# Two PEER layers on one core: routing weights through a DRAM table instead of one-hot products

## The chip, the cores and the metric

One core of one Trainium2 chip runs the whole network as a single program. The metric is the device time of that program in microseconds (us). The engines are TensorE (PE, matrix products into PSUM), VectorE (DVE), ScalarE (ACT), GpSimd (POOL) and SyncE (SP, which only issues transfers); sixteen DMA engines move data between DRAM and the on-chip memory. Each engine runs its own instructions in order and waits on semaphores that others raise.

## The reference, cut to what matters

The network has six large blocks. The change touches the two PEER blocks (`l` = 0 and 1), each a layer of 16384 one-neuron experts of which every token uses 8 x 16:

```python
# 256 tokens, d = 1024, 8 heads, 128 x 128 = 16384 experts, top 16
s1 = einsum('phd,nd->phn', q[..., :half], subkeys[0])
s2 = einsum('phd,nd->phn', q[..., half:], subkeys[1])
v1, i1 = top_k(s1, 16);  v2, i2 = top_k(s2, 16)
cs, ci = top_k((v1[..., :, None] + v2[..., None, :]).reshape(..., 256), 16)
e = take(i1, ci // 16) * 128 + take(i2, ci % 16)        # expert number
g = softmax(cs)                                          # routing weight
a = gelu(einsum('pd,phkd->phk', xb, u_tab[e]))
y = einsum('phk,phkd->pd', g * a, v_tab[e])
```

Neither kernel gathers experts. Both compute the products of every token with all 16384 rows of `u_tab`, apply gelu, multiply by a table of routing weights that is zero for experts not chosen, and multiply the result by all of `v_tab`.

## The kernel before

**The stream.** The tables come from DRAM as slabs of 128 x 2048 floats (1 MB, two halves or tiles of 512 KB), in the order of a fixed plan: among others `gla_v`, `gla_og`, `gla_out` (4 slabs each), `peer_q0` (8), `u0` (64), `v0` (64), and later the same for layer 1. SP loads them into a ring of two slabs; a half is loaded again once its low part has been made (semaphore `lo_made`). One u slab holds 2 x 128 experts, one v slab likewise.

**Products in parts.** Each tile is split into a high and a low part: ACT makes `split_hi` (L1562), DVE or POOL makes `split_lo` = tile - high (L1587 or L1575). PE multiplies high x high, high x low and low x high. There are two buffers of each part, so a maker can be two tiles ahead of PE at most.

**The u stage, 64 slabs.** For slabs 0 to 31 POOL makes the low parts, because DVE is choosing experts at that time (`peer_choose_vector`): the top 16 of each key half, of their sums, the expert numbers, the softmax. PE's lines are L1505 and L1509. For slabs 32 to 63 DVE makes the low parts and PE runs L1529 and L1533; the two halves of each product are copied out by ACT (L1628), added by DVE (L1877, `u_sum_vector`) and put through gelu by ACT. The results fill `gate`, 128 partitions x (128 key rows x 256 tokens).

**The routing weights.** They are built for groups of 8 tokens. DVE compares the chosen key numbers with all key numbers (L1831, L1833: one-hots of rows and columns) and multiplies the row one-hots by the weight in three bf16 parts (L1837, three instructions). PE multiplies column one-hots by weighted row one-hots (`routes_group_tensor`, L1948: 8 tokens x 3 parts = 24 matmuls of 64 columns), into PSUM. DVE multiplies that into `gate` (`routes_merge_vector`, L1848). 32 groups build the first 64 key rows, one group in each of u slabs 32 to 63; 32 more build the other 64 rows, one in each of v slabs 0 to 31.

**The v stage, 64 slabs.** For each tile ACT makes `gate_hi` (L1559) and `split_hi`, DVE makes `gate_lo` (L1585) and `split_lo` (L1587), and PE adds 12 matmuls of 512 columns (L2003). In slabs 32 to 63 DVE also computes four strips of modulation vectors for later blocks from 512 KB loads that POOL issues (`strip_chunk_vector`, L356; loads L395, two buffers `mod_w`), one chunk per slab nearly.

**Who waits for whom.** PE waits on ACT and DVE by counters (`hi_made`, `lo_made`, `gate_lo_made`), they on PE (`hi_free`, `lo_free`).

Of the kernel before, what the change touches and what calls it, by code (L numbers as in the profile page):

```python
# [29 lines left out]
I32 = mybir.dt.int32  # L30
# [11 lines left out]
RING = 2  # L42
BANK = 512
# [79 lines left out]

TWO_PI = 6.283185307179586
# [5 lines left out]
def build(nc, io, marks):  # L130

    new_marks = {}
    with ExitStack() as ctx:
# [40 lines left out]
        iota = sb("iota", [P, P])  # L174

# [70 lines left out]
        banks_free = sem("routes_banks_free")  # L246
# [15 lines left out]
        hot_rows, hot_cols = sem("hot_rows"), sem("hot_cols")  # L262
        hot_equal = sem("hot_equal")
        mlp_drained, mlp_squared, hid_made = sem("mlp_drained"), sem("mlp_squared"), sem("hid_made")
        routes_full = sem("routes_full")
# [773 lines left out]
        def constants_gpsimd(g):  # L1039
            for buf, val in ((ident, 0.0), (ones, 1.0), (zeros, 0.0), (band, 0.0), (after, 0.0),  # L1040
                             (blockm, 0.0), (upper, 1.0), (gmask_f, 1.0)):
                nc.gpsimd.memset(buf[:, :], val).then_inc(gpsimd_steps, g.step())
            nc.gpsimd.iota(iota[:, :], pattern=[[1, P]], base=0, channel_multiplier=0,
# [366 lines left out]
        peer_qT = gate[:, 80 * SEQ:(80 + 2 * PEER_H) * SEQ].rearrange("p (g n) -> p g n", g=2 * PEER_H)  # L1410
        A = Area(small)
        e_sel = A.take(3, NT, HK)
        top_v = A.take(2 * PEER_H, TOPK)
        top_if = A.take(2 * PEER_H, TOPK)
        top_i = A.take(2 * PEER_H * TOPK).bitcast(U32).rearrange("p (a b) -> p a b", b=TOPK)
        cand = A.take(TOPK * TOPK)
        cand2 = A.take(TOPK * TOPK)
        c_i = A.take(HK).bitcast(U32)
        c_part = A.take(HK).bitcast(U32)
        c_pf = A.take(HK)  # L1420
        match = A.take(4, TOPK, TOPK)
# [3 lines left out]
        HALF = KEYS // 2  # L1425
        GROUP = 8
        W_PARTS = 3

        def take_bf16(*shape):
            n = int(np.prod(shape))  # L1430
            ap = B.take(n // 2).bitcast(BF16)
            return ap.rearrange("p (a b) -> p a b", a=shape[0]) if len(shape) == 2 else ap
        PAIR = 2
        selT = take_bf16(2 + W_PARTS, SEQ * PAIR).rearrange("p n (t q) -> p n t q", q=PAIR)
        keys_bf = take_bf16(1, KEYS)[:, 0, :]
        hot_c = [take_bf16(GROUP, KEYS) for _ in range(2)]
        hot_r = [[take_bf16(GROUP, HALF) for _ in range(W_PARTS)] for _ in range(2)]
        w_left = B.take(SEQ)
# [38 lines left out]
        def peer_score_tensor(t, l):  # L1477
# [37 lines left out]
            with t.eng.Fori(0, 3) as i:  # L1515
                for j in range(8):
                    u_slab(i, j)
            for j in range(6):
                u_slab(3, j)
            peer_turn_tensor(t, l)  # L1520
            for j in range(6, 8):
                u_slab(3, j)
# [25 lines left out]
            with t.eng.Fori(4, 8) as i:  # L1548
                routed(i)
# [14 lines left out]
        def split_lo_gpsimd(g, name, i0, i1):  # L1564


            g.eng.wait_ge(lo_made, i0 * 8 + TILE0[name])
            with g.eng.Fori(i0, i1) as i:
                for j in range(4):
                    slot = (START[name] + j) % RING  # L1570
                    for e in range(2):
                        tile = TILE0[name] + 2 * j + e
                        g.eng.wait_ge(hi_made, i * 8 + (tile + 1))
                        g.eng.wait_ge(lo_free, i * 8 + (tile + 1))
                        nc.gpsimd.tensor_tensor(split_lo[:, e, :], ring[:, slot, e * D:(e + 1) * D],  # L1575
                                                split_hi[:, e, :].bitcast(F32), ALU.subtract).then_inc(lo_made, 1)
            g.seen.clear()
# [12 lines left out]
        def peer_score_scalar(a, l):  # L1590
# [44 lines left out]
            def late_step(i, first):  # L1635
                for j in range(8):
                    for e in range(2):
                        split_hi_scalar(a, f"u{l}", i, j, e, 8)
                    if j == 0 and first:
                        drain(i - 1, 7)  # L1640
                        continue
                    if j >= 2 or not first:
                        late_gelu(i if j >= 2 else i - 1, (j - 2) % 8)
                    late_copy(i if j else i - 1, (j - 1) % 8)

            def step(i, first=False):
                for j in range(8):
                    for e in range(2):
                        if j or not first:
                            split_hi_scalar(a, f"u{l}", i, j, e, 8)  # L1650
                    if j:
                        drain(i, j - 1)
                    elif not first:
                        drain(i - 1, 7)
                    if j == 4 and isinstance(i, int) and i == 3:
                        a.wait_ge(*when(f"chosen{l}"))
                        w = e_sel[:, 2, :, :].rearrange("p a b -> p (a b)")
                        nc.scalar.activation(w, w, ACT.Exp).then_inc(scalar_steps, a.step(f"weights{l}.exp"))
# [1664 lines left out]
```

## Time and profile before

| | us |
|---|---|
| median of 3 runs (2586.33 to 2589.01) | 2588.92 |
| span of the profiled execution | 2591.7 |
| PE busy | 2514.7 (97%) |
| DVE busy | 2119.7 (82%) |
| ACT busy | 1220.0 (47%) |
| POOL busy | 468.9 (18%) |

The profiled execution's span is 2.8 us above the median of the runs, 0.1%. A busy PE is not a PE at its peak, since its matmuls overlap in a pipeline; what a stage costs is read from the distance between the starts of its slabs. The granted PE clock is 1.00 in all stages from 60 us on that are shown below.

### The profile page before, as it was taken

Reading aid. Unit: us, or ns where it says so; the run is one execution under the profiler, and the core shown is the slowest. Engines: PE = TensorE matmul, PEld = TensorE weight load, DVE = VectorE, ACT = ScalarE, POOL = GpSimd, SP = SyncE. Lnnn points to the kernel's source line nnn. Section 1 sums busy time; section 2 is a strip of 40 time slices with the busy share of each in tenths; the row PEclk is TensorE's granted clock in tenths of the full one; section 3 lists DMA queues with packets and bytes.
Section 4 is the critical chain, followed back from the end, with each engine's and each line's share of the span. In section 5 each row is a group of like instructions: output and inputs, shape, how many; then the busy total and the mean of one; then the engine's idle time right before and its main releaser. Section 6 shows DMA issues by size and latency. Waiting matters only on the chain.

```text
span 2591.7 us, 48983 instructions
## 1 busy us (share of the span) xinstructions
PE 2514.7 (97%) x17184; PEld 2192.0 (85%) x17184; DVE 2119.7 (82%) x3783; ACT 1220.0 (47%) x1769; POOL 468.9 (18%) x385
## 2 busy tenths in 40 slices
PE   5999999999999999999999999999999999999998
PEld 4789999888888877899998888887878789777987
DVE  7889997888888778869978888887777788777754
ACT  4544444545444545444444554444545554334543
POOL 2115992000000001018980000000101000110000
PEclk8999999999999999999999999999999999999999
DMA  9775555555456887365555445546887567964554
GB/s 345 259 263 168 179 178 172 166 166 185 169 167 211 284 271 272 130 220 171 183 179 166 162 166 185 170 168 231 282 286 256 189 222 262 318 242 163 171 183 149
DMA packets 147831, 538.38 MB, mean 208 GB/s; under 512 B 16609, under 2 KB 16865, under 8 KB 147442
## 3 DMA queue, kind: packets, MB, share of 16 engines
q1 hardware_dynamic: 114226, 414.78, 46.9%
q0 software_dynamic: 32752, 119.24, 13.2%
q10 hardware_dynamic: 720, 2.62, 0.3%
q8 instruction: 79, 1.29, 0.2%
q14 instruction: 54, 0.44, 0.1%
HBM read 533.42 MB, written 3.15 MB: 207 GB/s over the span
## 4 chain that ended last, share of the span: by engine, by line
PE 83%; DVE 7%; POOL 3%; issue 3%; DMA 2%; ACT 2%; SPq 0%; DVEq 0%; POOLq 0%; ACTq 0%
PE ps L2003 26%; PE ps L1529 9%; PE ps L2748 7%; PE ps L748 6%; PE ps L1505 6%; PE ps L1457 5%; PE ps L1533 5%; PE ps L2730 5%; PE ps L1948 3%; PE ps L1509 3%; POOL split_lo L1575 3%; PE ps L2734 2%; DVE gate L928 1%; DMA gate<-in_mod 1%; PE ps L2142 1%
## 5 line engine op out<-in xcount | busy, mean ns | idle before, releaser
L1562 ACT ACTIVATE split_hi<-ring 128x1024 fp32r<-128x1024 f32 x760 | 801.0, 1056 | 757.8 <-PE ps L1509 199.8
L1587 DVE TENSOR_TENSOR split_lo<-ring,split_hi 128x1024 fp32r<-128x1024 f32 x572 | 698.5, 1222 | 177.0 <-ACT split_hi L1562 172.2
L1575 POOL TENSOR_TENSOR split_lo<-ring,split_hi 128x1024 fp32r<-128x1024 f32 x128 | 339.9, 2672 | 91.2 <-ACT split_hi L1562 90.9
L1559 ACT ACTIVATE gate_hi<-gate 128x256 fp32r (+1 forms) x252 | 105.4, 418 | 405.4 <-PE ps L2003 398.9
L2003 PE MATMUL ps<-split_hi,gate_hi 128*128 128x512 f32 x1024 | 285.1, 398 | 1.5 <-DVE gate_lo L1585 1.5
L2003 PE MATMUL ps<-split_hi,gate_lo 128*128 128x512 f32 x1024 | 278.2, 392 | 5.1 <-DVE gate_lo L1585 5.0
L2003 PE MATMUL ps<-split_lo,gate_hi 128*128 128x512 f32 x1024 | 278.0, 391 | 0.0
L1505 PE MATMUL ps<-h_parts,split_hi 128*128 128x256 f32 x2048 | 266.9, 283 | 0.0
L1529 PE MATMUL ps<-h_parts,split_hi 128*128 128x512 f32 x1024 | 261.6, 397 | 0.0
L1505 PEld LDWEIGHTS ps<-h_parts,split_hi 128*128 128x128 f32 x2048 | 254.9, 192 | 0.0
L2003 PEld LDWEIGHTS ps<-split_hi,gate_lo 128*128 128x128 f32 x1024 | 192.6, 189 | 48.4 <-DVE gate_lo L1585 7.5
L2003 PEld LDWEIGHTS ps<-split_lo,gate_hi 128*128 128x128 f32 x1024 | 191.8, 188 | 43.6 <-DVE split_lo L1587 3.3
L2003 PEld LDWEIGHTS ps<-split_hi,gate_hi 128*128 128x128 f32 x1024 | 187.7, 189 | 40.6 <-ACT split_hi L1562 2.8
L1529 PEld LDWEIGHTS ps<-h_parts,split_hi 128*128 128x128 f32 x1024 | 183.5, 189 | 32.7
L1585 DVE TENSOR_TENSOR gate_lo<-gate,gate_hi 128x256 fp32r<-128x256 f32 x252 | 106.8, 424 | 113.7 <-ACT split_hi L1562 112.2
L395 POOL DMA_DIRECT2D mod_w<-in_mod x64 | 33.8, 528 | 694.7 <-DVE strip_part L356 688.8
L1533 PEld LDWEIGHTS ps<-h_parts,split_lo 128*128 128x128 f32 x1024 | 139.7, 190 | 10.2
L1509 PE MATMUL ps<-h_parts,split_lo 128*128 128x256 f32 x1024 | 145.1, 284 | 2.0 <-POOL split_lo L1575 2.0
L436 POOL DMA_DIRECT2D small<-in_mod x104 | 55.1, 530 | 490.5 <-DVE modc L356 459.9
L1533 PE MATMUL ps<-h_parts,split_lo 128*128 128x256 f32 x1024 | 142.5, 282 | 0.0
L1837 DVE TENSOR_TENSOR small<-small 128x512 bf16<-128x512 bf16 x384 | 139.7, 421 | 0.0
L356 DVE CUSTOM_DVE_ANT_0 small<-small,gate,cols 128x1024 f32<-128x1024 f32 x104 | 131.9, 1280 | 6.1 <-DMA small<-in_mod 6.1
(405 smaller groups left out, 3951.0 us busy)
## 6 DMA issues: line engine op xcount, KB each, us to landing
ring<-in_stream SPq DMA_DIRECT2D x776, 512.0 KB, 4.3
small<-in_mod POOLq DMA_DIRECT2D x104, 512.0 KB, 5.6
mod_w<-in_mod POOLq DMA_DIRECT2D x64, 512.0 KB, 5.2
gate<-in_mod POOLq DMA_DIRECT2D x44, 512.0 KB, 6.9
gate<-in_mod SPq DMA_DIRECT2D x8, 512.0 KB, 16.2
gate<-in_mod ACTq DMA_DIRECT2D x4, 512.0 KB, 8.3
x_kept<-x POOLq DMA_DIRECT2D x8, 256.0 KB, 3.9
gate<-x_kept POOLq DMA_DIRECT2D x4, 512.0 KB, 8.5
```

The source lines that it names most:

```text
L356: return nc.vector.tensor_tensor_reduce(out=w, in0=w, in1=c_act, scale=1.0, scalar=start, op0=ALU.mult, op1=ALU.add, accum_out=out)
L748: return nc.tensor.matmul(ps[:, banks[2 * nb + i], :], src[:, b * per + n, i * P:(i + 1) * P], w[:, b % 2, at_:at_ + BANK], start=(b == n ...
L1505: nc.tensor.matmul(out, split_hi[:, e, c * P:(c + 1) * P], part[:, c, :], start=(part is hT_hi and c == 0), stop=False)
L1509: ins = nc.tensor.matmul(out, split_lo[:, e, c * P:(c + 1) * P], hT_hi[:, c, :], start=False, stop=(c == DC - 1))
L1529: nc.tensor.matmul(ps[:, bank, :].rearrange("p (a n) -> p a n", a=2), split_hi[:, e, c * P:(c + 1) * P], h_parts[:, :, c, :], start=(c == ...
L1533: ins = nc.tensor.matmul(ps[:, bank, SEQ:2 * SEQ], split_lo[:, e, c * P:(c + 1) * P], hT_hi[:, c, :], start=False, stop=(c == DC - 1), ski ...
L1562: nc.scalar.activation(split_hi[:, e, :], ring[:, slot, e * D:(e + 1) * D], ACT.Copy).then_inc(hi_made, 1)
L1575: nc.gpsimd.tensor_tensor(split_lo[:, e, :], ring[:, slot, e * D:(e + 1) * D], split_hi[:, e, :].bitcast(F32), ALU.subtract).then_inc(lo_m ...
L1587: nc.vector.tensor_tensor(split_lo[:, e, :], ring[:, (START[name] + j) % RING, e * D:(e + 1) * D], split_hi[:, e, :].bitcast(F32), ALU.sub ...
L1837: ins = nc.vector.tensor_tensor(pairs(hot_r[r][m]), equal, of_token(2 + m, HALF), ALU.mult)
L2003: return nc.tensor.matmul(ps[:, 2 * nb + n, :], g[:, e, n * P:(n + 1) * P], w[:, e, nb * BANK:(nb + 1) * BANK], start=opens, stop=True, sk ...
L2748: return nc.tensor.matmul(ps[:, 4 + 2 * nb + n, :], h[:, c0, n * P:(n + 1) * P], w[:, e, nb * BANK:(nb + 1) * BANK], start=(first and h is ...
```

## The change

The weights no longer come from one-hots. For each layer there is a table in DRAM of 128 x 128 experts x 256 tokens (16.8 MB).

- **Clearing.** SP writes zeros from `u_part` into the tables, 16 transfers of 1 MB for each: table 0 between the loads of `gla_v`, `gla_og`, `gla_out` and `peer_q0`, table 1 between the first 34 slabs of `u0`, one after each pair of slabs.
- **Choosing.** DVE chooses in four batches of two heads (both token tiles), not in two of eight. A class `UTiles` puts DVE's low parts between the pieces of choosing by a count of microseconds: no tile in the first 33, then one for each 1.4 (1.0 from tile 64 on). POOL makes the low parts of slabs 0 to 5 only. ACT does the exponentials at slabs 6, 15, 27 and 41 (`EXP_AT`).
- **Adding.** As soon as a batch has weights and row numbers, POOL issues 64 indirect transfers for it (2 heads x 2 token tiles x 16 ranks), each of 128 single floats, one per token, added to the table at the row that an index column in on-chip memory gives. A head waits until the adds of the head before it on the same token tile have landed. 256 of them in each layer.
- **Reading back.** POOL loads the first four slabs of weights (256 KB each), ACT issues the others in the v stage, four ahead. DVE multiplies one slab of weights into `gate` for each v slab, one slab ahead of its use.
- **Strips.** The modulation chunks are spread over the v stage, one for every other slab from slab 2 on.
- PE's one-hot products, DVE's one-hots, the turning of the chosen numbers on PE and the PSUM merges are gone.

The diff, cut to its core:

```diff
+POOL_SLABS, HEAD_START = 6, 33.0
+EXP_AT = [6, 15, 27, 41]
+CLEARS = 16
+FIRST_CLEARS = [START["gla_v"], START["gla_og"], START["gla_out"]]
...
-            def routed(i):
+            def paired(i):
                 for j in range(8):
-                    routes_group_tensor(t, i * 8 + (2 * l * GROUPS + j - GROUPS), j % 2)
...
+        def routes_gpsimd(g, l):
+
+            g.eng.wait_ge(routes_cleared[l], 16 * CLEARS)
+            routes = io["routes"][l].rearrange("a p t -> (a p t)").unsqueeze(1)
+            for b in range(BATCHES):
+                g.wait_ge(*when(f"weights{l}.{b}"))
+                for hh in range(PER):
+                    for i in range(NT):
+                        head = (l * BATCHES + b) * PER + hh
+                        g.wait_ge(routes_added[i], 16 * TOPK * head)
+                        for k in range(TOPK):
+                            n = (i * PER + hh) * TOPK + k
+                            g.eng.indirect_dma_start(
+                                out=routes,
+                                out_offset=bass.IndirectOffsetOnAxis(ap=r_index[:, b, n:n + 1].bitcast(U32), axis=0),
+                                in_=r_weight[:, b, n:n + 1], in_offset=None, compute_op=ALU.add) \
+                                .then_inc(routes_added[i], 16)
+            for i in range(NT):
+                g.wait_ge(routes_added[i], 16 * HK * (l + 1))
+            for slab in range(ROUTE_RING):
+                g.eng.dma_start(route_in[slab], routes_of(l, slab)).then_inc(first_routes_landed, 16)
...
+        class UTiles:
...
+            def after(self, us):
+
+                self.spent += us
+                while self.spent > 0:
+                    share = HEAD_START if self.tile == 2 * POOL_SLABS else 1.4 if self.tile < 64 else 1.0
+                    if self.tile == 2 * POOL_SLABS and self.spent < share:
+                        return
+                    self.one()
+                    self.spent -= share
...
+        def routes_merge_vector(v, l, slab):
+
+            if slab < ROUTE_RING:
+                v.wait_ge(first_routes_landed, 16 * ROUTE_RING * (l + 1))
             else:
...
+                v.wait_ge(route_landed[slab % ROUTE_RING], 16 * (15 * l + slab // ROUTE_RING))
+            v.wait_ge(u_drained, 68 * l + 4 + slab + 1)
+            dst = gate[:, 2 * slab * SEQ:(2 * slab + 2) * SEQ]
+            nc.vector.tensor_tensor(dst, dst, route_in[slab % ROUTE_RING].rearrange("p a t -> p (a t)"), ALU.mult) \
+                .then_inc(routes_merged, 1)
...
+            for slab in range(1, 64):
+                a.wait_ge(routes_merged, 64 * l + slab + 1)
+                if slab + ROUTE_RING < 64:
+                    route_load_scalar(a, l, slab + ROUTE_RING)
                 for e in range(2):
...
+                    if a == START["u0"]:
+                        with sp.Fori(1, 1 + CLEARS) as i:
+                            pair(i)
+                            clear_routes(1, i - 1)
```

How the instructions stand. First PE, in the second half of the u stage, one slab with what stands around it, before (`ps` is PSUM, `h_parts` the tokens' activations, `small` the one-hots):

```order
L1948 MATMUL ps<-small 128x64 x24
L1527 ISA
L1529 MATMUL ps<-h_parts,split_hi 128x512 x8
L1533 MATMUL ps<-h_parts,split_lo 128x256 x8
L1527 REGISTER_ALU
L1529 MATMUL ps<-h_parts,split_hi 128x512 x8
L1533 MATMUL ps<-h_parts,split_lo 128x256 x8
L1943 REGISTER_ALU
```

and now:

```order
L1526 MATMUL ps<-h_parts,split_hi 128x512 x8
L1530 MATMUL ps<-h_parts,split_lo 128x256 x8
L1524 REGISTER_ALU
L1526 MATMUL ps<-h_parts,split_hi 128x512 x8
L1530 MATMUL ps<-h_parts,split_lo 128x256 x8
L1538 REGISTER_ALU
```

The 24 small matmuls are gone from the slab; the 32 large ones stay as they were. The same 24 are gone from v slabs 0 to 31.

Second, POOL in the u stage of layer 0, from its last low part on. Before (the end of the loop that makes 64 tiles; `c_loop` belongs to the strips):

```order
L1575 TENSOR_TENSOR split_lo<-ring,split_hi 128x1024
L1573 REGISTER_ALU
L1575 TENSOR_TENSOR split_lo<-ring,split_hi 128x1024
L1568 REGISTER_ALU
L1568 COMPARE_AND_BRANCH
L321 DMA c_loop<-c_kept 128x1024
```

and now (with what each waits for; `routes0` is the table, `small` holds the weights):

```order
L1568 TENSOR_TENSOR split_lo<-ring,split_hi 128x1024 [waits lo_free,hi_made,lo_made] x12
L1583 DMA routes0<-small 4194304x1 [waits vector_steps,routes_cleared0]
L1583 DMA routes0<-small 4194304x1 x31
L1583 DMA routes0<-small 4194304x1 [waits routes_added_tile0]
L1583 DMA routes0<-small 4194304x1 x15
L1583 DMA routes0<-small 4194304x1 [waits routes_added_tile1]
L1583 DMA routes0<-small 4194304x1 x15
L1583 DMA routes0<-small 4194304x1 [waits routes_added_tile0,vector_steps]
...
L1591 DMA small<-routes0 128x2x256 [waits routes_added_tile1,routes_added_tile0]
```

The strips' first transfer, and four loads of weights on which the first v slab waits, now stand behind 256 adds.

Third, DVE in one of the first v slabs, before:

```order
L1831 TENSOR_TENSOR small<-small 128x512
L1833 TENSOR_TENSOR small<-small 128x1024
L1837 TENSOR_TENSOR small<-small 128x512 x3
L1585 TENSOR_TENSOR gate_lo<-gate,gate_hi 128x256
L1587 TENSOR_TENSOR split_lo<-ring,split_hi 128x1024
L1585 TENSOR_TENSOR gate_lo<-gate,gate_hi 128x256
L1587 TENSOR_TENSOR split_lo<-ring,split_hi 128x1024
L1848 TENSOR_TENSOR gate<-gate,ps 128x64x8
```

and now, in a slab with a strip chunk (the two L364 rows):

```order
L1858 TENSOR_TENSOR gate<-gate,small 128x512
L1605 TENSOR_TENSOR gate_lo<-gate,gate_hi 128x256
L1607 TENSOR_TENSOR split_lo<-ring,split_hi 128x1024
L1605 TENSOR_TENSOR gate_lo<-gate,gate_hi 128x256
L1607 TENSOR_TENSOR split_lo<-ring,split_hi 128x1024
L364 ISA mod_w,strip_part<-mod_w,c_loop 128x1024
L364 ISA strip_part 128x1
```

Five one-hot instructions are gone, the merge reads on-chip memory and stands ahead of the slab's low parts, and half of the slabs carry a strip chunk.

## Rows read from the trace of the kernel before

**Rows 1.** The page's span and busy time of each engine (share, instructions).

```profile
span 2591.7 us, 48983 instructions
PE 2514.7 (97%) x17184; PEld 2192.0 (85%) x17184; DVE 2119.7 (82%) x3783; ACT 1220.0 (47%) x1769; POOL 468.9 (18%) x385
```

**Rows 2.** The chain that ended last, early u slabs of layer 0 (start us, us, what).

```profile
220.72 1.91 PE ps L1505 x16
...
223.59 1.92 PE ps L1505 x16
...
226.47 1.92 PE ps L1505 x16
```

**Rows 3.** The same chain, first and last of the 32 late u slabs.

```profile
409.08 1.92 PE ps L1529 x8
...
606.86 1.92 PE ps L1529 x8
```

**Rows 4.** The same chain, v slabs with a group (620.19 to 802.07) and without.

```profile
620.19 5.57 PE ps L2003 x24
...
802.07 5.54 PE ps L2003 x24
808.33 33.47 PE ps L2003 x144
```

**Rows 5.** The same chain, the end of v in layer 0, the second half in layer 1.

```profile
990.64 1.56 PE ps L2003 x5
...
1755.68 16.56 PE ps L2003 x72
...
1777.84 7.78 DMA mod_w<-in_mod
...
1942.74 1.56 PE ps L2003 x5
```

**Rows 6.** Groups by line and shape (busy us, mean ns, idle before it).

```profile
L1587 DVE TENSOR_TENSOR split_lo<-ring,split_hi 128x1024 fp32r<-128x1024 f32 x572 | 698.5, 1222 | 177.0 <-ACT split_hi L1562 172.2 <-issue 2.4 <-PE ps L748 1.8
L1585 DVE TENSOR_TENSOR gate_lo<-gate,gate_hi 128x256 fp32r<-128x256 f32 x252 | 106.8, 424 | 113.7 <-ACT split_hi L1562 112.2
L1877 DVE TENSOR_TENSOR u_part<-u_part,ps 128x512 f32<-128x512 f32 x64 | 44.0, 688 | 0.4 <-ACT u_part L1628 0.4
L356 DVE CUSTOM_DVE_ANT_0 mod_w<-mod_w,c_loop 128x1024 f32<-128x1024 f32 x64 | 77.9, 1220 | 13.6 <-DMA mod_w<-in_mod 13.6
L1948 PE MATMUL ps<-small 128*128 128x64 bf16 x3072 | 111.8, 193 | 0.5 <-DVE small L1837 0.5
```

**Rows 7.** POOL's instructions by line, ns min/median/max, and its transfers in a row (timeline).

```profile
L395 POOL DMA_DIRECT2D mod_w<-in_mod x64: 527/527/530, 615.5 to 1928.6; - x64
L342 POOL DMA_DIRECT2D pos_i<-in_pos x1: 547/547/547, 28.7 to 28.7; - x1
L1575 POOL TENSOR_TENSOR split_lo<-ring,split_hi x64: 2370/2422/3433, 218.8 to 403.0; 128x1024 fp32r<-128x1024 f32 x64
33.38 4.17 POOL L369 DMA_DIRECT2D gate<-in_mod  x8 [2.51 <-DVE modc L356]
```

**Rows 8.** POOL's stores of x to DRAM (L3156, 256 KB each).

```profile
DMA to landing us min/median/max: 2.7/3.9/5.9
```

**Rows 9.** Busy time by stage (engines us and instructions, PE clock, DMA share, GB/s).

```profile
20.00:60.00 40.00, 30.65 (x176) 24.19 (x175) 32.75 (x52) 21.20 (x27) 8.45 (x16) 0.79 0.98 363
60.00:100.00 40.00, 39.86 (x207) 33.31 (x207) 36.42 (x44) 21.91 (x26) 4.23 (x8) 1.00 0.76 259
220.00:408.00 188.00, 187.00 (x1548) 185.67 (x1547) 167.91 (x447) 88.06 (x103) 168.75 (x64) 1.00 0.54 178
408.00:612.00 204.00, 204.00 (x1793) 181.12 (x1792) 175.42 (x283) 102.89 (x128) 0.00 (x0) 1.00 0.51 166
808.00:992.00 184.00, 181.40 (x795) 146.25 (x791) 141.94 (x204) 88.91 (x130) 16.88 (x32) 1.00 0.81 277
```

**Rows 10.** Transfers of the weight stream, KB each, median us to landing.

```profile
ring<-in_stream SPq DMA_DIRECT2D x776, 512.0 KB, 4.3
```

More of the change, by code:

```diff
@@ L1424, in build @@
         B = Area(small)
[L1425 to L1438, printed above, removed]
+        route_in = [B.take(2, SEQ) for _ in range(ROUTE_RING)]
         assert B.at <= 4224
@@ L1513, in u_slab @@
                     ins.then_inc(lo_free, 1)
-            with t.eng.Fori(0, 3) as i:
+            with t.eng.Fori(0, 4) as i:
                 for j in range(8):
                     u_slab(i, j)
[L1518 to L1522, printed above, removed]
             def paired_tile(i, j, e):
@@ L1562, in split_hi_scalar, with split_lo_gpsimd @@
             nc.scalar.activation(split_hi[:, e, :], ring[:, slot, e * D:(e + 1) * D], ACT.Copy).then_inc(hi_made, 1)
[L1564 to L1577, printed above, removed]
+        def split_lo_gpsimd(g, name, slabs):
+            for j in range(slabs):
+                for e in range(2):
+                    tile = TILE0[name] + 2 * j + e
+                    g.wait_ge(lo_made, tile)
+                    g.wait_ge(hi_made, tile + 1)
+                    g.wait_ge(lo_free, tile + 1)
+                    nc.gpsimd.tensor_tensor(split_lo[:, e, :], ring[:, (START[name] + j) % RING, e * D:(e + 1) * D],
+                                            split_hi[:, e, :].bitcast(F32), ALU.subtract).then_inc(lo_made, 1)
@@ new lines, in peer_choose_vector, with __init__, one, through @@
+            paced = UTiles(v, l)
+            for b in range(BATCHES):
+                choose_batch_vector(v, l, b, paced)
+            paced.through(EXP_AT[BATCHES - 1] + 1)
+            weights_vector(v, l, BATCHES - 1)
+            paced.through(64)
+        class UTiles:
+            def __init__(self, v, l):
+                self.v, self.l, self.tile, self.spent = v, l, 2 * POOL_SLABS, 0.0
+            def one(self):
+                v, l, (slab, e) = self.v, self.l, divmod(self.tile, 2)
+                if self.tile == 2 * POOL_SLABS:
+                    v.wait_ge(lo_made, TILE0[f"u{l}"] + 2 * POOL_SLABS)
+                split_lo_vector(v, f"u{l}", slab // 8, slab % 8, e)
+                if e and slab > 32:
+                    u_sum_vector(v, l, (slab - 33) // 8, (slab - 33) % 8)
+                self.tile += 1
+            def after(self, us):
[6 more added lines that the diff above has]
+                    self.spent -= share
+            def through(self, slab):
+                while self.tile < 2 * slab:
+                    self.one()
@@ new lines, in choose_batch_vector @@
+            nc.vector.scalar_tensor_tensor(out=c_pf, in0=e_part[:, 0, :], scalar=float(KEYS), in1=e_part[:, 1, :],
+                                           op0=ALU.mult, op1=ALU.add).then_inc(vector_steps, v.step())
+            v.wait_ge(vector_steps, v.n)
+            for i in range(NT):
+                cut = slice(i * PER * TOPK, (i + 1) * PER * TOPK)
+                nc.vector.tensor_scalar(r_index[:, b, cut], c_pf[:, cut], float(SEQ), token[:, i:i + 1],
+                                        ALU.mult, ALU.add).then_inc(vector_steps, v.step())
@@ L2049, in peer_out_scalar @@
                     table_ahead_scalar(a, ACT.Sqrt)
-            for first, last in ((1, 4), (4, 8)):
-                a.eng.wait_ge(banks_free, (2 * l + 1 + first // 4) * GROUPS + 2)
-                with a.eng.Fori(first, last) as i:
-                    for j in range(8):
-                        for e in range(2):
-                            split_hi_scalar(a, f"v{l}", i, j, e, 8)
             a.seen.clear()
@@ L3115, in _ @@
                             .then_inc(slab_landed[s % RING][e], 16)
+                    if a in FIRST_CLEARS:
+                        if not FIRST_CLEARS.index(a) and s == a:
+                            sp.wait_ge(*when("constants"))
+                        clear_routes(0, 4 * FIRST_CLEARS.index(a) + s - a)
+                    if a == START["peer_q0"]:
+                        for q in range(2):
+                            clear_routes(0, 12 + 2 * (s - a) + q)
                 if a == START["qa"]:
@@ L3119, in _, with pair @@
                 if end - a > 4:
-                    with sp.Fori(1, (end - a) // RING) as i:
+                    def pair(i):
                         for j in range(RING):
```

374 lines of the change are left out of this document (156 added, 218 removed).

## The prediction

> **What bounds the kernel now.** I read the page first: PE is busy for 2514.7 of 2591.7 us, every other engine less [rows 1]. So only what PE executes or waits for can change the time, and I went on to the chain that ended last, which is PE nearly throughout the two PEER blocks, and read the cost of each stage from the distance between the starts of equal pieces. In the early u stage a tile takes 2.88 us (223.59 to 226.47), a slab 5.76 [rows 2]. In the late u stage, where each slab carries a one-hot group, 31 slabs take 606.86 - 409.08 = 197.78 us, 6.38 each [rows 3]. In the v stage with groups 29 slabs take 181.88 us, 6.27 each; behind it six slabs without groups take 33.47, 5.58 each [rows 4]. The duration of one of the 3072 small matmuls, 193 ns [rows 6], is no price: they overlap.
>
> A last reading is the second half of v. From 808.33 to 992.20 (990.64 + 1.56) it takes 183.9 us in layer 0, and from 1755.68 to 1944.30, 188.6 us in layer 1 [rows 4, 5], where 32 x 5.58 = 178.6 were due, plus one and two small products for later vectors of 1.7 each, which I leave at 2 and 3. So some 3 and 7 us are waits; the chain of layer 1 shows one of them as a strip load of 7.78 us [rows 5].
>
> **What goes.** The groups: (6.38 - 5.76) x 32 = 19.8 us in u and (6.27 - 5.58) x 32 = 22.1 in v, 41.9 in each layer, **83.8 us** in both. That the remaining products keep their pace needs PE's partners to keep up, which I check below. The waits of the second half of v: strip loads will come for every second slab, so each has twice the time; of the 10 us I take 6.
>
> **What DVE gets.** In u it must make 116 low parts at 1.222 us (142 us) and 32 sums at 0.688 (22) [rows 6], and choose. Choosing can't cost more than DVE's whole busy time while it chose, 167.9 us [rows 9], so at most 332 us in a stage of 128 x 2.88 = 369. That hides it, at 90%: in the list of instructions one low part follows each 1.4 us of choosing, 2.6 us in a tile of 2.88. The cover is thin; were it gone, each tile would be late by the excess. In v DVE has 2 x (0.424 + 1.222) = 3.29 us of parts, a merge that I price as the sum of the same shape, 0.69 (that one reads PSUM, the merge does not), and in every second slab a chunk of 1.22: 5.2 us at most of 5.58. Hidden. ACT, busy for less than half of the late u stage [rows 9], issues one load more in each v slab. Hidden.
>
> **What POOL gets: the disputed term.** Weights of the four batches stand in DVE's order behind tiles 16, 40, 63 and 90 of 128 (counted in the list of instructions). With 2.88 us a tile from 220.7, that is 267, 336, 402 and 480 us; u ends at 589. Before it the last adds must land (2.7 to 5.9 us as POOL's stores do [rows 8]), four loads must land (4.3 [rows 10]), and DVE and ACT must merge and split: some 10 us, so the adds must be issued by 579. From the first batch on that allows (579 - 267) / 256 = **1.22 us for each add**; from the others 1.27, 1.38 and 1.55. The trace of before has no indirect transfer. Lower bound: a direct transfer occupies POOL for 0.527 us [rows 7], also with 16 bytes for each of 128 partitions (0.547). Upper bound: one at a time, as fast as the fastest store lands, 2.7 us [rows 8]. I take 1.0, about twice the direct row, since the descriptor work is of that row's kind (128 pieces) with 128 row numbers to read and apply; it is nearer to that row than to the landing, because eight direct transfers were issued in 4.17 us without a wait for their landing [rows 7]. At 1.0 the last adds are issued at 480 + 64 = 544: hidden with 35 us to spare. At 0.53 nothing changes further. At 2.7 they end at 267 + 691 = 958, and the first v slab comes 379 us late in each layer.
>
> The Trainium skill has a rule against this: SBUF — State Buffer, section "SBUF: two separate sides", says that VectorE can lock GpSimd out of a port that they share and that transfers issued by GpSimd then wait for their descriptors. The trace does not show it for direct transfers: 64 issues took 527 to 530 ns [rows 7], the strip loads among them beside a DVE that was busy for 77% (141.94 of 184) [rows 9]. It does show POOL and DVE in each other's way where POOL reads on-chip memory: its low part took 2370 at best and 3433 at worst [rows 7]. An add reads an index column there, so the row leaves the question open; the price is a rival below.
>
> **What the DMA engines get.** In late u the stream takes a share of 0.51 at 166 GB/s [rows 9], so 325 GB/s at full share, which is 0.2 us for a 4 KB row on one of 16 engines. An add is 8 single floats and, I assume, one completion on each engine. Bounds for one: nothing (by its bytes) and 0.2 us (as a full row). A float is far nearer to nothing; I take 30 ns, 0.27 us for each add on each engine, which fits the free 0.49. It decides from 0.49 / 9 = 54 ns on. A clear of 1 MB takes 3.2 us of all engines at the same rate. Table 1's sixteen stand in SP's queue between the loads of the next slabs, one per 11.5 us: share 0.28, total 0.79, and a load has some 8 us between the low part that frees its half and its use; now it lands in 4.3 [rows 10]. Bounds 0 and 10 us; I take 3, once. Table 0's first eight come beside a share of 0.76 at 60 to 100 us [rows 9]: their 8.4 MB need 23 us at the best rate shown (363 GB/s [rows 9]) and find less than 15 free in the two stages. Bounds 0 and 12; I take 5. Reading back adds 16.8 MB over 357 us, 47 GB/s, while strips fall to half their rate: below the 277 GB/s of the second half now. Hidden. The first merge now stands between the end of the adds and the first v slab: 1 us in each layer.
>
> **Sum.** -83.8 - 6 + 5 + 3 + 2 = -79.8. The profiled execution's span lies 2.8 us above the median of the runs, and the difference is taken off the median: 2588.9 - 79.8 = 2509, forecast **2510 us**.
>
> **The rivals.**
> - *Adds a little late.* Between 1.22 and 1.37 us for each, POOL eats part of the gain: at 1.30 it ends 256 x 1.30 - 312 = 21 us late per layer, 2510 + 42 = 2552 us. For it: twice the direct row is no measurement. At 1.37 the gain is gone.
> - *POOL becomes the bound: slower.* The place is the joint of u and v, where PE waits for the first merge; the price is 256 times the excess over 1.22 us, in each layer. At 1.5: 72 x 2 = 144, so 2510 + 144 = 2654 us. Against it: the direct rows are a third of that.
> - *Each add waits for DVE's instruction.* Half of a 1.22 us low part, for 90% of the time, on top of 1.0: 1.55 us, 85 late per layer, 2680 us. For it: the stretched low parts of POOL; against it: the 64 even issues. This is the rule of the skill's SBUF page named above.
> - *The DMA engines become the bound: slower.* At 100 ns for each small piece an add costs 0.9 us on each engine, 230 us per layer; with the stream's 0.51 x 312 = 159 us that is 389 us in 312, 77 late per layer, 2664 us, whether the adds or the stream are late. For it: pieces of four bytes that are read, added and written back; against it: nothing but their size.
> - *DVE is late.* If the thin cover fails by 0.3 us in the 78 tiles from 12 to 90, 23 us per layer, 2556 us. It would show as PE waiting for `split_lo` in the u stage.
> - *No change* would need two of these to cancel the gain by chance: 83.8 us of PE's work do go.
>
> **Chances.** Forecast 0.56 (own range 2496 to 2535: all waits gone and no cost of clearing, 2588.9 - 83.8 - 10 = 2495; clears at their upper bounds, 2524, and some 10 us of small waits); adds a little late 0.09; DVE late 0.06; POOL the bound 0.11; the lock 0.07; the DMA engines 0.11. Within 0.2% (5 us, about what a measurement of this kernel can tell from no change) falls a narrow strip of the first rival. So faster 0.69, same 0.02, slower 0.29. The range runs from 2495 to 2665: beyond its top lie the lock and the worse half of POOL and DMA as bounds, some 0.17, below it almost nothing.
>
> **What the profile after would show.** Slabs of 5.76 us in late u and 5.58 throughout v, no line of small matmuls; adds on POOL of about 1.0 us each, the last before 550 us in layer 0's old time (some 5 us later by the clears); no wait of DVE for the first read back. PE waiting at the joint, with POOL still adding, would prove the adds too slow; if POOL's instructions are short but its semaphore waits for landed adds are long, or ACT waits for the ring, it is the DMA engines. Waits of PE for `split_lo` in u would prove DVE late. In the `gla_v` and `gla_og` stages ACT waiting for the ring by more than 12 us would prove the clears dearer than I think. The prediction is wrong if adds take more than 1.37 us, or a small piece on a DMA engine more than 54 ns.

## The result, and the profile after

The changed kernel takes **2972.66 us** (median of 4 runs, 2971.88 to 2973.3) against 2588.97 us (2586.33 to 2591.22) before: a ratio of 1.148, interval 1.1466 to 1.1499. 2510 was forecast, 2495 to 2665 as the range. The kernel became slower by 384 us, and the forecast was wrong by 463 us.

The page of the changed kernel, to be read against [rows 1]: its span, the engines' busy time, and the groups of the adds (L1583) and of DVE's merge (L1858), with busy time, mean ns of one, and idle time before with what ended it.

```profile
span 2970.3 us, 40708 instructions
PE 2418.6 (81%) x14100; PEld 2116.9 (71%) x14100; DVE 1933.4 (65%) x3297; ACT 1235.5 (42%) x1787; POOL 1130.0 (38%) x803
...
L1583 POOL DMA_INDIRECT routes<-small x512 | 933.3, 1823 | 190.5 <-issue 157.5
...
L1858 DVE TENSOR_TENSOR gate<-gate,small 128x512 f32<-128x512 f32 x128 | 87.5, 685 | 473.4 <-DMA small<-routes 473.4
```

PE has 96 us less work, as it was meant to, and DVE 186 less. No engine is busy for the whole span any more: PE's 81% leave 552 us in which it does nothing. Where they lie, the chain that ended last shows (start, us, what), in the last late u slab of layer 0 and at the joint of u and v:

```profile
420.08 1.84 PE ps L1526 x8
...
425.67 1.84 PE ps L1526 x8
...
431.26 1.84 PE ps L1526 x8
...
599.24 233.85 issue
833.09 13.68 PE ps L1966 x48
```

The late u slabs are 5.59 us apart (6.38 in [rows 3]). Then PE stands still for 234 us before its first v product; layer 1 has a second such gap. "issue" names no releaser, so the waits of the other engines must name it (us in total, times, longest):

```profile
PE ps L1966 <- issue: 470.1, 2, 236.3
...
DVE gate L1858 <- DMA small<-routes: 473.4, 2, 237.9
```

DVE waits twice for the first weights read back, and PE behind it. Those loads stand on POOL behind the adds. POOL's timeline (start, us, instruction, idle before it) shows the adds while DVE makes low parts, then alone, then their end and the four loads; under it DVE's low parts beside the first of them:

```profile
588.59 2.49 POOL L1583 DMA_INDIRECT routes<-small  x1 [0.31 <-issue]
591.38 2.49 POOL L1583 DMA_INDIRECT routes<-small  x1 [0.30 <-issue]
594.17 2.49 POOL L1583 DMA_INDIRECT routes<-small  x1 [0.30 <-issue]
596.96 1.55 POOL L1583 DMA_INDIRECT routes<-small  x1 [0.30 <-issue]
598.82 1.55 POOL L1583 DMA_INDIRECT routes<-small  x1 [0.30 <-issue]
...
821.73 1.55 POOL L1583 DMA_INDIRECT routes<-small  x1 [0.30 <-issue]
825.42 2.98 POOL L1591 DMA_DIRECT2D small<-routes  x4 [2.13 <-DMA routes<-small]
```

```profile
588.42 1.23 DVE L1607 TENSOR_TENSOR split_lo<-ring,split_hi 128x1024 fp32r<-128x1024 f32 x1 [1.57 <-ACT split_hi L1558]
...
591.22 1.22 DVE L1607 TENSOR_TENSOR split_lo<-ring,split_hi 128x1024 fp32r<-128x1024 f32 x1 [0.90 <-ACT split_hi L1558]
...
594.01 1.22 DVE L1607 TENSOR_TENSOR split_lo<-ring,split_hi 128x1024 fp32r<-128x1024 f32 x1 [1.57 <-ACT split_hi L1558]
```

An add that is alone takes 1.55 us, and 0.30 pass before the next: 1.86 us from start to start. Beside the low parts of these last u tiles one add takes 2.49 and the starts are 2.79 apart, exactly one for each u tile. The mean over all 512 is (933.3 + 157.5) / 512 = **2.13 us** from start to start. Put into the prediction's own formula, 256 x (2.13 - 1.22) = 233 us for each layer: the gap of 234. The window's two ends had both moved, and by about the same: the first add starts at 279.0 us, not at 267, and u ends at 599, not at 589.

### The profile page after: what moved, and what is told of

It reads as the page before. It is cut to its first block, busy times and chain, and to the rows that moved or that the text cites. A ratio compares the mean times of both kernels' runs of the same rounds, so it can differ in the third digit from the quotient of the medians.

```text
span 2970.3 us, 40708 instructions
## 1 busy us (share of the span) xinstructions
PE 2418.6 (81%) x14100; PEld 2116.9 (71%) x14100; DVE 1933.4 (65%) x3297; ACT 1235.5 (42%) x1787; POOL 1130.0 (38%) x803
## 3 DMA queue, kind: packets, MB, share of 16 engines
q1 hardware_dynamic: 131122, 448.34, 44.2%
## 4 chain that ended last, share of the span: by engine, by line
PE 70%; issue 17%; DVE 9%; DMA 3%; ACT 2%; SPq 0%; POOL 0%; DVEq 0%; ACTq 0%
PE ps L1966 23%; PE ps L1526 8%; PE ps L1507 7%; PE ps L2707 6%; PE ps L1459 5%; PE ps L756 5%; PE ps L1530 4%; PE ps L2689 4%; PE ps L1511 3%; PE ps L2693 2%; DMA ring<-in_stream 1%; DVE gate L936 1%; ACT split_hi L1558 1%; DVE split_lo L1607 1%; PE ps L2101 1%
## 5 line engine op out<-in xcount | busy, mean ns | idle before, releaser
L1583 POOL DMA_INDIRECT routes<-small x512 | 933.3, 1823 | 190.5 <-issue 157.5
L1607 DVE TENSOR_TENSOR split_lo<-ring,split_hi 128x1024 fp32r<-128x1024 f32 x676 | 823.9, 1220 | 262.8 <-ACT split_hi L1558 256.1
L1858 DVE TENSOR_TENSOR gate<-gate,small 128x512 f32<-128x512 f32 x128 | 87.5, 685 | 473.4 <-DMA small<-routes 473.4
L403 POOL DMA_DIRECT2D mod_w<-in_mod x64 | 33.9, 530 | 623.2 <-DVE strip_part L364 623.2
L1555 ACT ACTIVATE gate_hi<-gate 128x256 fp32r<-128x256 f32 x252 | 105.8, 420 | 346.5 <-PE ps L1966 346.5
L1688 ACT ACTIVATE gate_hi<-gate 128x256 fp32r<-128x256 f32 x4 | 1.4, 408 | 472.5 <-DVE gate L1858 472.5
```

Source lines behind the costliest of these rows:

```text
L1583: g.eng.indirect_dma_start(out=routes, out_offset=bass.IndirectOffsetOnAxis(ap=r_index[:, b, n:n + 1].bitcast(U32), axis=0), in_=r_weight[ ...
L1607: nc.vector.tensor_tensor(split_lo[:, e, :], ring[:, (START[name] + j) % RING, e * D:(e + 1) * D], split_hi[:, e, :].bitcast(F32), ALU.sub ...
```

## The experiments

Two theories stood against each other after the result. *Price:* an add costs POOL 1.86 us by itself, and this alone breaks the window of 1.22. *Lock:* what breaks it is DVE's two-operand instructions, which hold POOL up. A third suspect was the DMA engines, with their 4-byte pieces. The kernels x1 to x6 are the changed kernel with the edit that is shown; what they compute is therefore incomplete. x3, x4 and x5 were run once and have no interval, but their differences of 124 to 354 us are far beyond the 1.4 us between the four runs of the changed kernel.

**x1: no adds.**

```diff
-                for hh in range(PER):
-                    for i in range(NT):
...
-                            g.eng.indirect_dma_start(
...
-            for i in range(NT):
-                g.wait_ge(routes_added[i], 16 * HK * (l + 1))
```

> The changed kernel with all 512 indirect adds left out; the tables stay zero, clearing, choosing, reading back and merging stay, so the PEER output is zero. If POOL's adds are the bound at the joint of u and v, both stalls there (234 us each in the changed kernel's chain) vanish and the time is 2972.7 - 468 = 2505 us, a little less where the clock had fallen. If the clears, the read-backs or the DMA engines carry the loss, much of the 384 us over the kernel before stays: 2600 us or more.

Measured: 2501.63 us (2499.39 to 2503.33), 0.9666 of before (0.965 to 0.9682). Clears, choosing, reading back and merging are all still there; so the adds cost 471 us, more than the whole loss of 384, and everything else came out 8 us better than forecast.

**x2: half of the adds.**

```diff
-                        for k in range(TOPK):
+                        for k in range(TOPK // 2):
```

> Half of the adds left out (8 of the 16 ranks of every head and token tile, 128 instructions per layer instead of 256; the weights of the other ranks are missing). If the number of adds times their price sets the end, 32 adds of the last batch from about 483 us on at 2.8 us each end at 573, before u ends at 599: no stall, 2505 to 2515 us, the same as without adds. If a fixed wait (a landing, the read-back, the clear) held the joint, a stall of some tens of us would stay in each layer.

Measured: 2500.27 us (2491.32 to 2506.03), 0.9659 (0.9629 to 0.969). With 128 adds in each layer no time is lost at all; the chain passes from u to v without a gap, and the adds' group shows a longer mean, since none of them has POOL to itself after u:

```profile
L1583 POOL DMA_INDIRECT routes<-small x256 | 525.1, 2051 | 111.3 <-issue 78.3
```

```profile
595.97 0.95 PE ps L1530 x8
596.93 1.40 PE ps L1966 x6
598.34 9.85 PE ps L1966 x42
```

A cost that were the same for each add would have left half of the 471 us. There is a threshold, as the prediction had it: 128 x (525.1 + 78.3) / 256 = 302 us fit into the 312 of the window.

**x3: DVE's low parts in u take one operand from PSUM.** The high part is replaced as an operand by two PSUM banks, so that DVE reads on-chip memory once.

```diff
-                split_lo_vector(v, f"u{l}", slab // 8, slab % 8, e)
...
+                nc.vector.tensor_tensor(split_lo[:, e, :], ring[:, (START[f"u{l}"] + slab) % RING, e * D:(e + 1) * D],
+                                        ps[:, 6:8, :].rearrange("p a n -> p (a n)"), ALU.subtract).then_inc(lo_made, 1)
```

> All adds stay, but DVE's low parts of the u stage subtract a stale piece of PSUM instead of the high part (wrong numbers, same size and about the same duration), so these DVE instructions have one operand in on-chip memory instead of two. If DVE's two-operand instructions stretch the adds, an add takes 1.86 us from start to start in u as well, they end at about 279 + 475 = 754 us instead of 824, and the time is 2972 - 2 x 70 = 2830 us. If the adds are long in u because the DMA engines are busy with the stream, or because a head waits for landed adds, they stay at 2.3 us there and the time stays near 2972.

Measured: 2848.16 us in one run, 124 less than the changed kernel. The adds' group, and the gap:

```profile
L1583 POOL DMA_INDIRECT routes<-small x512 | 806.9, 1576 | 191.5 <-issue 159.7
```

```profile
597.10 171.88 issue
```

The mean falls from 1823 to 1576 ns, nearly that of an add alone, while DVE's low parts last as long as before (median 1.22 us in both). So DVE's second operand in on-chip memory does hold POOL up, and costs some 62 us of the 234 in each layer (70 were expected). It isn't what decides: without it 172 us remain.

**x4: plain writes in place of adds.** A table entry that two heads choose then holds the later weight alone.

```diff
-                                in_=r_weight[:, b, n:n + 1], in_offset=None, compute_op=ALU.add) \
+                                in_=r_weight[:, b, n:n + 1], in_offset=None) \
```

> The adds become plain indirect writes (no addition; where two heads chose one expert for one token the later weight replaces the earlier). If POOL's work on 128 row numbers is the price, start to start stays 1.86 us alone and the time 2972. If the addition is what costs POOL, the cycle falls towards the direct transfer's 0.53 and the time by up to 2 x 256 x 1 us. On the DMA engines the share at the stall (0.23) should fall if an addition takes more there than a write.

Measured: 2618.64 us in one run, 354 less than the changed kernel. The group, the gap, and two writes that are alone:

```profile
L1583 POOL DMA_INDIRECT routes<-small x512 | 575.3, 1124 | 194.7 <-issue 161.3
```

```profile
601.00 56.82 issue
```

```profile
609.72 0.97 POOL L1583 DMA_INDIRECT routes<-small  x1 [1.71 <-issue]
610.99 0.97 POOL L1583 DMA_INDIRECT routes<-small  x1 [0.30 <-issue]
```

An indirect write holds POOL for 0.58 us less than an add, and at 1.27 us from start to start it already misses the window by itself, by 256 x (1.27 - 1.22) = 13 us in each layer. The 1.71 stands at the change from one head to the next; the profile names no releaser for it. The DMA engines have less to do as well. The windows' row (its end is PE clock, DMA share, GB/s) and the DMA view of the writes that are alone, 610 to 650 and 610 to 646 us:

```profile
610.00:650.00 40.00, 0.00 (x0) 0.00 (x0) 0.00 (x0) 0.00 (x0) 29.66 (x31) 0.50 0.02 0
```

```profile
DMA packets 896, 0.02 MB, mean 0 GB/s; under 512 B 896, under 2 KB 896, under 8 KB 896
```

The share is 0.02, where the adds that are alone have 0.23 (the row stands further down), and a write has 32 pieces (896 in 36 us, 28 writes), where an add has 144. So x4 takes away the addition and most of the pieces together; how the 0.58 us divide between the two it doesn't tell.

**x5: 64 of the 128 rows in each add.**

```diff
-                                out_offset=bass.IndirectOffsetOnAxis(ap=r_index[:, b, n:n + 1].bitcast(U32), axis=0),
-                                in_=r_weight[:, b, n:n + 1], in_offset=None, compute_op=ALU.add) \
+                                out_offset=bass.IndirectOffsetOnAxis(ap=r_index[0:64, b, n:n + 1].bitcast(U32), axis=0),
+                                in_=r_weight[0:64, b, n:n + 1], in_offset=None, compute_op=ALU.add) \
```

> All 512 indirect adds stay, but each carries 64 partitions instead of 128 (the weights of half of the tokens are missing). If an add has a price for each row, its 1.55 us fall to about half and the time by 2 x 256 x 0.75 us or until the adds are hidden: 2505 to 2650 us. If the price is fixed for each instruction, it stays at 1.55 + 0.30 and the time near 2972.

Measured: 2835.89 us in one run, 137 less than the changed kernel. The group, the gap, one add that is alone, and three adds beside DVE's last low parts in u:

```profile
L1583 POOL DMA_INDIRECT routes<-small x512 | 792.1, 1547 | 191.1 <-issue 157.8
```

```profile
603.39 161.55 issue
604.36 1.39 POOL L1583 DMA_INDIRECT routes<-small  x1 [0.30 <-issue]
```

```profile
593.19 1.87 POOL L1583 DMA_INDIRECT routes<-small  x1 [0.30 <-issue]
595.37 1.40 POOL L1583 DMA_INDIRECT routes<-small  x1 [0.30 <-issue]
597.07 1.39 POOL L1583 DMA_INDIRECT routes<-small  x1 [0.30 <-issue]
```

Half of the rows save 0.16 us of 1.55. Most of the price is one for the instruction: 1.39 + 0.30 with half of its work. Neither side of the expectation gave the time, though: 0.16 x 512 is 82 us, and 137 were gained. The rest comes from a smaller stretch beside DVE: three of the shorter adds fit into two u tiles (593.19 to 598.77), and only one of the three is stretched, where in the changed kernel each add of this stretch is (2.49). The adds that are alone follow each other with the same 0.30 between, with half of the pieces to move; so nothing in the trace points at the DMA engines as what sets the pace.

The gaps of the five kernels agree with one formula, with the mean start-to-start time from each one's own group and the window of 312 us. The means come from the same traces, so the table tests the window and the place, not the price:

| | mean, us | adds in a layer | formula, us | gap, us |
|---|---|---|---|---|
| changed kernel | 2.130 | 256 | 233 | 233.85 |
| x2 | 2.357 | 128 | below 0 | none |
| x3 | 1.888 | 256 | 171 | 171.88 |
| x4 | 1.439 | 256 | 56 | 56.82 |
| x5 | 1.855 | 256 | 163 | 161.55 |

**x6: no adds, no clears,** and weights read back from the stream's array, so that the transfers of reading back remain.

```diff
-                sp.dma_start(dst, no_routes).then_inc(routes_cleared[l], 16)
-            return io["routes"][l][2 * slab:2 * slab + 2].rearrange("a p t -> p a t")
+            return io["stream"][START[f"v{l}"] + slab, :, 0:2 * SEQ].rearrange("p (a t) -> p a t", a=2)
```

> No adds and no clears, and the read-back loads take 256 KB from the weight stream's array instead of the table (wrong weights). Against the kernel without adds this prices the clears alone: the u stage of layer 0 began 8.4 us later in the changed kernel than before, so 8 us less than without adds, some 2497 us. If the 16 clears inside u0 also cost, more than 10 us less; if clears cost nothing and the 8 us came from elsewhere, no difference.

Measured: 2489.82 us (2484.88 to 2495.51), 0.9614 (0.9595 to 0.9634), 12 us under x1. ACT's waits for the stream (us in total, times, longest), in x1 and then in x6:

```profile
ACT split_hi L1558 <- DMA ring<-in_stream: 33.9, 15, 6.8
```

```profile
ACT split_hi L1558 <- DMA ring<-in_stream: 7.1, 4, 4.8
```

The stretch from 60 to 100 us by windows (last three columns: PE clock, DMA share, GB/s), again x1 and then x6:

```profile
60.00:100.00 40.00, 39.15 (x203) 32.66 (x203) 35.75 (x45) 20.71 (x25) 4.22 (x8) 1.00 1.01 389
```

```profile
60.00:100.00 40.00, 39.84 (x206) 33.49 (x205) 36.97 (x46) 21.25 (x25) 4.53 (x9) 1.00 0.78 268
```

The clears fill the DMA engines in the `gla` stages, and the stream is late there: the first product of u starts at 230.5 us in x1 and at 219.6 in x6. The sixteen clears beside u show no price: from its first product to the first of v, u takes 369.0 us in x1 and 370.4 in x6, although the 12 us of difference are more than the 10 from which the expectation would have blamed them.

**x7: the kernel before, with its strip chunks spread.** 8 of the 32 chunks of each layer stand in v slabs that have a one-hot group, the others in three of four later slabs.

```diff
+                    for s in range(8, 32):
+                        routed_slab_vector(v, name, l, s // 8, s % 8, False)
+                        if s >= 9 and s % 3 == 0:
+                            chunk((s - 9) // 3)
```

> The kernel before with one part of the change alone: the strip chunks spread (8 in every third of v slabs 9 to 30, 24 in three of four of slabs 32 to 63, instead of one in nearly every slab of 32 to 63); one-hots as before. If the 10 us of waits in the second half of v are loads that come too fast after one another, they go: 2579 to 2583 us. If DVE has no room for a chunk beside the one-hots in the first half, PE waits there instead: 2589 or up to 2600 us.

Measured: 2595.59 us (2590.21 to 2600.36), 1.0023 (1.001 to 1.0036): slower by 0.2%. DVE's strip chunks in x7, to be read against their row in [rows 6], with 13.6 us of waits for loads:

```profile
L356 DVE CUSTOM_DVE_ANT_0 mod_w<-mod_w,c_loop 128x1024 f32<-128x1024 f32 x64 | 78.0, 1220 | 0.0
```

PE's waits in the kernel before, and in x7:

```profile
PE ps L2003 <- DVE gate_lo L1585: 6.5, 5, 3.3
```

```profile
PE ps L1959 <- DVE small L1837: 10.2, 18, 0.8
```

The waits for strip loads go, and PE waits 10.2 us for one-hots instead (0.5 before, L1948 in [rows 6]): DVE has too little room for a chunk beside a group.

**h1: half of each.** x2 shows that 128 adds cost no time, so this kernel computes everything and sends only the first 128 tokens through the table; the other 128 keep their one-hot groups, 16 in u slabs 48 to 63 and 16 in every second v slab up to 30. DVE chooses all heads of the first tokens before those of the others: a batch is now four heads (`PER`) of one token tile, and batches 0 and 1 are the first tile's. The table and its clears are half as large (`CLEARS` 8). `FIRST_GROUP` is 48, `GROUPS` 16; the strip chunks stand in v slabs 31 to 62. The edit, cut, against the changed kernel:

```diff
-        BATCHES, PER = 4, 2
+        BATCHES, PER = 4, 4
...
-            for b in range(BATCHES):
+            for b in range(2):
...
+            for i in (4, 5):
+                paired(i, False)
+            with t.eng.Fori(6, 8) as i:
+                paired(i, True)
...
+            for k in range(GROUPS):
+                routes_group_vector(v, 2 * l, k)
+                paced.through(FIRST_GROUP + k + 1)
+                if k:
+                    one_hot_merge_vector(v, 2 * l, k - 1)
...
+                if slab % 2 == 0 and slab < 32:
+                    routes_group_vector(v, 2 * l + 1, slab // 2)
...
+                if 31 <= slab < 63:
+                    strip_part_vector(v, l, slab - 31)
```

> The whole result is computed: token tile 0 gets its weights through the DRAM table (128 adds in each layer, heads in their order), token tile 1 by the one-hot groups of the kernel before (16 groups in u slabs 48 to 63, 16 in every second v slab up to 30), clears and reads back of half the size. Theory (the adds cost nothing as long as POOL is done with them before u ends): 128 adds at the mean cycle of 2.13 us of the changed kernel, begun at 267 us, take 273 us, and end at 540 of some 590; so PE doesn't wait at the joint, and what is gained is half of the groups: 16 x (6.38 - 5.59) + 16 x (6.27 - 5.58) = 23.7 us in each layer, 47 in both, less half of the table's clears, some 6: 2589 - 47 + 6 = 2548 us. Rival: with one token tile alone each head must wait for the landing of the head before it (8 x 2 to 3 us), and the one-hots keep VectorE busy for some 6.2 us of a slab in slabs 48 to 63, beside which an add takes 2.5 us or more; then the adds end after u, by 10 to 20 us in each layer, and the time is 2568 to 2590, with PE waiting at the joint behind POOL.

Measured: **2549.09 us** (2544.42 to 2550.68, 5 runs), 0.9834 of before (0.9816 to 0.9852): 1.7% less than the kernel before, and 14% less than the changed one. Its page, its adds (ns min, median, max), their end on POOL, and the chain at the joint:

```profile
PE 2466.2 (97%) x15642; PEld 2153.6 (85%) x15642; DVE 2056.2 (81%) x3683; ACT 1236.0 (49%) x1787; POOL 669.4 (26%) x545
```

```profile
L1629 POOL DMA_INDIRECT routes<-small x256: 1549/1734/2613, 272.6 to 1504.4; - x128
...
  DMA routes<-small: 51.3, 13
```

```profile
583.57 1.90 POOL L1629 DMA_INDIRECT routes<-small  x1 [0.30 <-issue]
587.40 2.25 POOL L1637 DMA_DIRECT2D small<-routes  x3 [1.93 <-DMA routes<-small]
```

```profile
604.83 0.95 PE ps L1552 x8
605.78 1.38 PE ps L2077 x6
607.16 0.03 issue
```

The rival's ingredients are there, each head's wait for the landing of the one before among them (51.3 us in 13 waits), but the loads of weights are issued by 589.65, 16 us before the first v product at 605.78, and PE doesn't wait. The theory gave the time within 1 us, but not the way there: its adds should have ended at 540 us and end at 585.47, 2.44 us for each from the first at 272.56 on. Some 20 us are left before the first v product, of the 50 that were expected, and the changed kernel needs 10 of them between its last add (823.28) and its first v product (833.09).

## Why the prediction was wrong, step by step

**The step that failed** is the price of one add: "I take 1.0, about twice the direct row, since the descriptor work is of that row's kind". It is 1.86 us from start to start alone (1.55 busy, 0.30 between) and 2.13 in the mean of this kernel. The direct transfers, 527 to 530 ns in [rows 7] and 530 in the mean after, were no likeness: x4 puts the indirect write without addition at 1.27, and the add at 0.58 more. The upper bound, 2.7, did hold for the mean; single adds in u reach 2.61 busy and 0.30 between. By the text's own formula the mean gives 2510 + 2 x 233 = 2976, within 4 us of the result: the place (the joint), the threshold (1.22) and the price of the excess were right, as x2 to x5 show. That it is as near as 4 us is in part luck: the rest of the kernel came out 8 us better than the 2510 (x1), and the slow start after each gap cost 2.5 us (below). The threshold held because both ends of the window came later alike: u starts at 228.9 us in place of 220.5 (see the clears below).

**The range** failed for a second reason. The rival "POOL becomes the bound" was worked out at 1.5 us, and the range reached 2665, while the text's own upper bound meant 256 x (2.7 - 1.22) = 379 us in each layer. A term with 512 instructions in it multiplies its doubt; the range should have gone to that end, or the chance for it should have been larger than 0.11.

**The lock** was a rival with a chance of 0.07, held against the even direct issues, and it is there for adds: 2.49 against 1.55 us, 62 us in each layer by x3. The rival had it right in kind, at half a low part on top of each add (0.55; measured 0.24 in the mean), but on a price that was too low. The Trainium skill (SBUF — State Buffer, section "SBUF: two separate sides") says that a VectorE instruction with two inputs in on-chip memory and a GpSimd instruction that reads on-chip memory exclude each other for the whole instruction; x3, which takes one input away, agrees with it. The stretched low parts of POOL in [rows 7], 3433 against 2370, were the row that pointed at it; what stretched those no run tested.

**The DMA engines** did not bind, but were nearer to it than the forecast had it. From 600 to 822 us in the changed kernel the adds are alone. The DMA view of this stretch counts their pieces, and the row of the windows (to 820) ends with PE clock, DMA share and GB/s:

```profile
DMA packets 17164, 0.08 MB, mean 0 GB/s; under 512 B 17163, under 2 KB 17163, under 8 KB 17163
```

```profile
600.00:820.00 220.00, 0.00 (x0) 0.00 (x0) 0.00 (x0) 0.00 (x0) 183.70 (x120) 0.51 0.23 0
```

0.23 x 222 us x 16 engines / 17163 pieces = 48 ns for one in the mean, against 30 taken and 54 as the decision. In 222 us at 1.86 there are 119 adds, so 144 pieces for each, 9 on each engine, as assumed. In u, beside the stream and the clears, the engines are nearly full: from 340 to 410 us the share is 0.96 (0.53 before, 0.82 in x1). Even that did not hold the adds: in x3 the share there is 1.01, and its 37 adds take 59.0 us, 1.6 for each.

**The groups** were worth more. In u the late slabs run at 5.59, not at the 5.76 of the early ones, so 0.79 x 32 = 25.3 us in place of 19.8. Over whole stages, from the first product of u to the first of v, u takes 391.9 us in either layer before, and 370.4 and 368.4 in x6: 45 less in both layers together, where 39.6 stood. The v stage, from its first product to its last, takes 382.4 and 387.2 us before, and 352.3 and 353.9 in x6: 63 less, where 44.2 for the groups and 6 for the strip waits stood. How the 63 divide between groups and waits no run tells. The four stages give 108, the whole profiled span of x6 is 101.5 shorter; 7 us are lost in other stages, and why is open.

**The clears** cost about 12 us (x1 against x6), where 5 and 3 stood. The first product of u starts 10.9 us later, where 5 stood for table 0, and table 1's clears, taken at 3, show no price. The sign that was named for dear clears came too: ACT waits 33.9 us for the ring in x1, 23.3 of them from 60 to 140 us, where 12 was the mark. The errors of size go both ways and cancel in part, which is luck: x1 came out at 2501.6, 8 under the forecast.

**DVE's cover** in u held. PE waits for a low part there twice, 7.1 us together in both layers (46 by the rival "DVE is late").

**After the gap** PE does not start at full speed: the granted clock is 0.51 in the stretch above, where PE did nothing, which is the lower of its two levels (1.2 of 2.4 GHz), and the first 48 products of v take 13.68 us, where x1, without a gap, needs 1.38 + 9.84. So some 2.5 us come on top of the gap; x3 to x5 show it too (13.63, 13.44 and 13.82).

Open is what POOL does in the 0.58 us that an add takes more than a write, and in the time that doesn't depend on the rows: a line through 1.55 us for 128 rows and 1.39 for 64 leaves 1.23 for none, an estimate from these two points. More rows for one instruction weren't tried.

## What to carry to other kernels

A price that the profile doesn't show and that is multiplied by some hundred instructions decides the sign by itself: work out the number at which it turns, and when the bounds lie on both sides of it, let the range reach the far end. The indirect transfers here were paid mostly by the instruction: half of the rows saved a tenth of the time. Count them against the window in which the issuing engine is free; what fitted into that window cost nothing (x2). So the best version need not be either kernel: move as much of the work as the idle engine can hide, and leave the rest where it was.

## What the runs showed of the hardware that was not expected

- An indirect add of 128 single floats holds GpSimd for 1.55 us and 0.30 more before the next; with 64 rows 1.39; a plain indirect write of 128 floats 0.97. A direct transfer of 512 KB holds it for 0.53.
- Beside VectorE's low parts, whose two operands lie in on-chip memory, the add takes 2.49 us in late u; with one of the operands in PSUM its median there is 1.55 (x3). The direct strip loads in the same kernel stay at 0.53 to 0.55.
- A piece of an add takes a DMA engine some 48 ns in the mean (worked out above), 144 pieces for 128 floats; a plain indirect write has 32 pieces, and the engines' share falls from 0.23 to 0.02.
